# Two of 36 modulation panels moved from the first stage to the routing stage of a two-block transformer kernel

## The reference, cut to what matters

```python
mod  = silu(c) @ w_ada + b_ada                  # block 1: 6 vectors of 1024 (shift, scale, gate, twice)
x   += gate1 * mixer(modulate(x, ...)) @ w_out  # attention heads and delta-rule heads side by side
h    = modulate(x, norm2_w, shift2, scale2)
l    = h @ w_router + b_router                  # 32 experts, the best 4 of each token, softmax weights
x   += gate2 * sum_over_chosen(weight * expert(h))      # expert: 1024 -> 2 x 1024 -> swiglu -> 1024
# block 2, two layers, each:
mod   = silu(c_2)  @ ada_w_2[i] + ada_b_2[i]    # 6 vectors of 1024, for the tokens
mod_c = silu(c_ctx) @ ada_w_2[i] + ada_b_2[i]   # the same weights, for the context rows
# then a mixer (retention; neighbourhood attention) and an MLP of 4096
```

## Time and profile before

| what | value |
| --- | --- |
| median of 3 runs | 2687.79 us (2685.8 to 2687.81) |
| the profiled execution | 2683.9 us |
| its span, first to last instruction | 2682.1 us |
| PE busy / PEld busy | 2512.1 us (94%) / 1846.0 us (69%) |
| DVE / ACT / POOL busy | 1308.6 us (49%) / 500.5 us (19%) / 25.7 us (1%) |
| bytes moved by DMA | 661.33 MB, mean 247 GB/s |
| mean granted TensorE clock | 0.975 |

### The profile page before, as it was taken

The page is one execution under the profiler, slowest core; times in us unless marked ns, Lnnn a source line. Parts: engine busy times, 40 slices in busy tenths (PEclk is TensorE's granted clock), DMA queues, the critical chain, the costliest instruction groups (busy, mean ns, idle before and its releaser), DMA issues.

```text
span 2682.1 us, 44817 instructions
## 1 busy us (share of the span) xinstructions
PE 2512.1 (94%) x18374; PEld 1846.0 (69%) x18374; DVE 1308.6 (49%) x2733; ACT 500.5 (19%) x684; POOL 25.7 (1%) x46
## 2 busy tenths in 40 slices
PE   6997989999999999999989999998999998997998
PEld 5886755655555555555567777776888887775897
DVE  2445543333333333333364535447655456776876
ACT  1111110000000000000022222232222213332442
POOL 0000000000000000000000000000000000000000
PEclk8998989999999999999989999998999999998999
DMA  8789779999999999999942122121322322322652
GB/s 341 293 310 348 299 300 420 422 422 422 422 422 422 422 422 422 422 422 422 421 185 90 63 79 79 63 94 63 111 94 94 98 89 81 119 93 87 220 188 78
DMA packets 94078, 661.33 MB, mean 247 GB/s; under 512 B 10513, under 2 KB 11169, under 8 KB 15985
## 3 DMA queue, kind: packets, MB, share of 16 engines
q1 hardware_dynamic: 89360, 642.10, 60.6%
q0 software_dynamic: 4608, 17.66, 2.0%
HBM read 658.66 MB, written 1.05 MB: 246 GB/s over the span
## 4 chain that ended last, share of the span: by engine, by line
PE 76%; DMA 11%; DVE 8%; issue 2%; SPq 2%; ACT 1%; DVEq 0%; ACTq 0%
PE bank L185 19%; PE bank L1809 9%; DMA diag_gtmp<-in_panels_e 9%; PE bank L1790 9%; PE bank L1677 6%; PE bank L1729 3%; PE bank L1663 3%; PE bank L1272 3%; PE bank L1129 2%; PE bank L1569 2%; DMA ring<-in_units_a 2%; PE bank L1550 2%; SPq L664 2%; PE bank L1708 2%; PE bank L1886 1%
## 5 line engine op out<-in xcount | busy, mean ns | idle before, releaser
L185 PE MATMUL bank<-ring,scratch 128*64 128x256 f32 x2176 | 249.8, 382 | 0.0
L185 PEld LDWEIGHTS bank<-ring,scratch 128*64 128x64 f32 x2176 | 150.2, 137 | 94.9 <-issue 26.2
L927 ACT ACTIVATE scratch<-scratch 128x256 f32<-128x256 f32 x68 | 28.3, 416 | 807.5 <-DVE scratch L2570 807.5
L2574 DVE TENSOR_SCALAR scratch<-bank 128x256 f32<-128x256 f32 x68 | 28.9, 425 | 225.3 <-PE bank L185 225.3
L2931 DVE TENSOR_TENSOR w_lo<-ring,w_hi 128x2048 fp32r<-128x2048 f32 x46 | 105.4, 2291 | 67.5 <-ACT w_hi L1019 67.3
L2570 DVE TENSOR_SCALAR scratch<-bank 128x256 f32<-128x256 f32 x68 | 28.9, 425 | 204.3 <-PE bank L185 204.3
L1790 PE MATMUL bank<-hT_hi,w_hi 128*128 128x512 f32 (+1 forms) x352 | 126.1, 358 | 0.8 <-ACT mtmp L1030 0.8
L185 PE MATMUL bank<-hT,scratch 128*64 128x256 f32 x1088 | 125.5, 381 | 0.0
L1809 PE MATMUL bank<-w_hi,hid_hi 128*128 128x512 f32 x320 | 124.6, 390 | 0.5 <-DVE hid_lo L2939 0.5
L1790 PE MATMUL bank<-hT_hi,w_lo 128*128 128x512 f32 (+1 forms) x352 | 125.1, 355 | 0.0
L1790 PE MATMUL bank<-hT_lo,w_hi 128*128 128x512 f32 (+1 forms) x352 | 125.1, 355 | 0.0
(11 more groups left out here) (544 smaller groups left out, 5147.1 us busy)
## 6 DMA issues: line engine op xcount, KB each, us to landing
ring<-in_panels_e SPq DMA_DIRECT2D x136, 1024.0 KB, 25.6
ring<-in_units_a SPq DMA_DIRECT2D x88, 1024.0 KB, 7.2
hid<-in_panels_e SPq DMA_DIRECT2D x68, 1024.0 KB, 25.3
hT<-in_panels_e SPq DMA_DIRECT2D x68, 1024.0 KB, 25.5
ring<-in_panels_m SPq DMA_DIRECT2D x64, 1024.0 KB, 5.2
yacc<-in_panels_e SPq DMA_DIRECT2D x34, 1024.0 KB, 25.5
diag_gtmp<-in_panels_e SPq DMA_DIRECT2D x34, 1024.0 KB, 26.2
rows<-in_panels_e SPq DMA_DIRECT2D x34, 1024.0 KB, 26.1
```

The source lines that it names most:

```text
L185: m = self.pe.matmul(b[s * rows:(s + 1) * rows, 0:cols], lhs(k), v[:, s * cols:(s + 1) * cols], start=(first and k == 0), stop=(k == KT - 1))
```

## The change

Panels 34 and 35 leave the first stage. All other panels there are taken two places earlier: panel 24 stands where 26 stood, 25 behind level 0, and so on. The two units of each late panel are put behind the units of the output product. The late products are made in the routing: 34 behind the logits, 35 behind the sums over `sel`; their turns come behind the turns of the gathered rows. On DVE, both copies into `arow` stand behind the weights of experts 0 and 1, and both additions to `modcol` behind the scaled rows. SP issues the four late units between expert panels 0, 2 and 4, and the expert panels in the order 0, 2, 4, 5, 1, 3, since slots 1 and 3 are the ring that the late units lie in. Before the output biases PE waits for banks 6 and 7.

```diff
+LATE = 2
@@ first_units
-    add_ada(ADA - 20)
-    return r + [("out", c, h, UNIT) for h in range(2) for c in range(2)]
+    add_ada(ADA - 20 - LATE)
+    r.extend([("out", c, h, UNIT) for h in range(2) for c in range(2)])
+    add_ada(LATE)
+    return r
@@ sync
-            for n, (_, _, _, words) in enumerate(order):
+            late = len(order) - 2 * LATE
+            for n, (_, _, _, words) in enumerate(order[:late]):
...
-            for used, value in ((b2_go, 1), (unit_used, len(order) - 2), (tiles_free, 1), (unit_used, len(order)),
-                                (rows_ready, XT), (tiles_free, 2)):
+
+            def first_panel(used, value, n):
                 sp.wait_ge(used, value)
-                panel(pe_[loads.n], loads, start=True)
+                for h in range(2):
+                    half_panel(pe_[n], n, h)
+                loads.n += 1
+
+            first_panel(b2_go, 1, 0)
+            for n in range(late, late + 2):
+                first_unit(n, UNIT)
+            first_panel(tiles_free, 1, 2)
+            for n in range(late + 2, late + 4):
+                first_unit(n, UNIT)
+            first_panel(rows_ready, XT, 4)
+            first_panel(tiles_free, 2, 5)
+            first_panel(unit_used, late + 2, 1)
+            first_panel(unit_used, late + 4, 3)
@@ tensor
-                if not more:
-                    ada_beside(24)
                 if i:
                     att_turn()
+            AD.read()
+            ada_turn(23, AD)
+            att_values(DN_HEADS - 1)
             ada_product()
-            AD.read()
-            ada_turn(24)
-            att_values(DN_HEADS - 1)
-            ada_before(26)
...
-                ada_before(27 + l)
+                ada_before(25 + l)
...
-            ada_before(34)
+            ada_before(32)
...
-            ada_before(35)
+            ada_before(33)
...
-            ada_turn(ADA - 1)
+            ada_turn(ADA - LATE - 1)
@@ tensor, routing
             S.close(pe.matmul(b[:, EXPERTS:2 * EXPERTS], logit_part[:, 1, :], stack[:, :], start=True, stop=True))
+            ada_product(AD)
             from_dve.get()
...
             S.close(pe.matmul(b[:, 2 * EXPERTS:3 * EXPERTS], ones[:, :], sel[:, 1, :], start=False, stop=True))
+            ada_product(AD)
             G.read()
...
                         pe.wait_ge(b2_in, 16)
+                        AD.read()
                         output_biases(0)
...
             S.read()
+            for j in range(ADA - LATE, ADA):
+                AD.read(1)
+                ada_turn(j, AD)
             fillers = (EG, ES, EA, EM)
@@ vector (the same renumbering, and)
             places((0, 1))
             weights((0, 1))
+            for j in range(ADA - LATE, ADA):
+                ada_product(j, AD)
             turned_gates()
             gathered(0)
             gathered(1)
+            for j in range(ADA - LATE, ADA):
+                ada_turn(j, AD)
             list_started()
```

More of the change, by code:

```diff
@@ L654, in _, with panel @@
         def _(sp):
-            def panel(src, panels, start=False):
+            def panel(src, panels):
                 for h, used in enumerate((E["half0"], E["done"])):
-                    if not start:
-                        sp.wait_ge(used, panels.at(1 - len(wide)))
+                    sp.wait_ge(used, panels.at(1 - len(wide)))
                     half_panel(src, panels.n % len(wide), h)
@@ L2385, in _ @@
                 level_part(p, 0).then_inc(level_ready[p], 1)
-            ada_product(25)
-            ada_turn(24)
+            ada_turn(23, AD)
             att_values(DN_HEADS - 1)
-            ada_before(26)
+            ada_product(24)
             A.settle()
@@ L2404, in _ @@
                     .then_inc(level_ready[p], 1)
-            ada_before(27)
+            ada_before(25)
             for l in range(1, LEVELS):
```

## The result

| | before | after |
| --- | --- | --- |
| median of 3 runs | 2687.79 us (2685.8 to 2687.81) | 2666.2 us (2663.91 to 2668.76) |
| profiled execution, its span | 2683.9, 2682.1 us | 2666.2, 2664.4 us |
| PE / DVE / ACT busy | 2512.1 / 1308.6 / 500.5 us | 2503.6 / 1308.2 / 500.3 us |
| mean granted clock | 0.975 | 0.979 |

The ratio of the runs is 0.9922, 95% interval 0.99 to 0.9945. Forecast was 2672.3 us in a range from 2667.5; measured is 2666.2, so the time lies 1.3 us outside the range on the fast side, and the gain is 21.6 us by the medians and 17.7 by the two profiled executions, for 15.5 forecast.

What follows compares the result with a forecast made beforehand. The experts' fixed DMA stream sets the end, so time won ahead of its issue at 364.24 us is won whole. 13.8 + 2.0 = 15.8, taken as 15.5; 2687.8 - 15.5 = 2672.3 us, range 2667.5 to 2679.5.

Steps and rivals of the forecast that it cites:

- the bound: Experts: streamed at a flat 422 GB/s, 984 us for 198 panels, so their end is the issue at 364.24 plus a constant.
- part 1: First stage without two panels: level 1's second half starts at 236.2 against 250.0, gain 13.8 us, bounds 12.1 to 14.4.
- The reading beside it: First stage near 222 us: panels take 2 us each at full clock and need 5 us of transfer each.
- Rival (a): First stage: only PE's work on two panels is saved, 4.4 us, giving 2683.4 us; chance 0.05.
- Rival (b): Ahead of the experts: the bytes bind, the load stream keeps its length, nothing changes, 2687.8 us; chance 0.04.
- part 2: Routing: the late panels delay little and raise PE's clock by about 350 us; net 2.0 us gained, bounds 1.3 lost to 3.6 gained.
- part 3: SP's queue and the ring: expert panels 1 and 3, issued later, still land in time under idle DMA; cost nothing.
- rival (c): Start of the experts: panels 1 and 3 come late, the kernel is slower, 2695 us at 40 us from issue; chance 0.04.
- the number and the range: Whole kernel: 2672.3 us from a 15.5 us gain on the median, range 2667.5 to 2679.5 us.

Runs made afterwards that it cites:

- e4: The kernel before with two blocks of 32 matmuls on constants (fillers) added in the routing; 2682.23 us against 2682.98, ratio 0.9997.
- e6: The kernel before with all matmuls, but the four units of panels 24 and 25 loaded as 32 KB instead of 1 MB; 2681.48 us, ratio 0.9987.
- e5: The kernel before with all loads, but 8 matmuls for 32 in panels 24 and 26; 2682.89 us against 2685.49, ratio 0.9988.
- e1: The changed kernel measured once more, nothing altered, beside the kernel before; 2668.86 us against 2682.98, ratio 0.9944.
- e12: The changed kernel measured a third time, nothing altered, in a later set on another chip; 2669.04 us against 2683.02, ratio 0.9949.
- e3: The changed kernel with panels 34 and 35 and their loads left out and 32 matmuls on constants in each of their routing places; 2667.42 us, ratio 0.994.
- e2: The changed kernel with panels 34 and 35 left out, with their loads, products, copies and turns, both routing places empty; 2671.47 us, ratio 0.996.
- e11: The changed kernel plus 32 matmuls on constants while ACT writes the first row features and 28 ahead of the first expert; 2664.3 us, ratio 0.994.

## Why the prediction was right and wrong

**Right: the bound.** The experts' stream is a constant. The table's column has 998.6 to 1001.5 us, and the issue of the second round's first half panel carries all that is won ahead of it. That step counted 984 us of transfer and the landing.

**Right: part 1 in size.** Forecast 13.8 us. By the two first profiles the logits came 12.9 us earlier. Part of the missing 0.9 us may be an earlier clock step: in the profile after, panel 21 took 2.70 us at 212, and PE waited 1.04 for panel 23's second unit. Two traces of the first stage of before (before and e4) have their logits at 345.2 in the mean, and the three of the changed kernel at 331.2: 14.0. Panel 25's second unit came at 235.4 for the 234.05 forecast, and full clock held, as taken.

**Right, and shown in part: why it is 13.8.** The sum walked through PE's instructions with the units' landing times held, and that was sound: up to there both kernels ask for the same units. The reading beside it, that panels need 5 us of transfer each, fits the kernel before, where the DMA share is 0.99 and 1.01 from 215 to 235 us and the 12.38 us of the earlier trace rows are the flight of one unit among four. It is not the whole: e6 took 4 MB away and won 3 us, because a unit is asked for only when its slot is free. Rival (a), only PE's work, fell with e5: its work was worth nothing at that place. Rival (b), the bytes, fell with the result, which moved no byte out: 15.5 us gained for none. The Trainium skill, "Perfetto Trace Analysis", Identifying the Most-Contended Engine, by which that rival's time would have come, does not hold over a whole span here. The Trainium skill, "Perfetto Trace Analysis", Optimization Strategy, speaks of kernels with several regimes, in which the most-contended engine changes; the trace before is of that kind: up to 350 us PE is busy for 303 us and the DMA moves 320 GB/s, in the experts the DMA share is 1.01 at 422 GB/s, and what was won lies ahead of the experts.

**Right: part 2, with its spread.** Forecast 2.0 us, bounds -1.3 to 3.6. The first profile showed 4.7, outside; the mean over six traces without and five with fillers is 2.7, inside. I had taken the clock to rise near 350 and the first expert to run at half: that is e1 and e12. The first profile after had full clock in both, the case I had set as an upper bound, with 1 us on top because panel 34 met the rising clock in its middle. That the mean lies so near the forecast is luck in part: the kernel before with the same fillers, e4, gained 1.1 us by the trace and 0.8 by the medians. The traces agree in direction with the Trainium skill, "TensorE: Matmul & The Clock Gate", Part 1, by which activity releases the half rate: e3 reached full clock in the routing and e2 did not before 347. That fillers pay for themselves is shown for e3 against e2 (4.0 us) and not for e4 against before (0.8 us, within the noise).

**Right: part 3.** Expert panels 1 and 3 were not late; PE came to `ring` at 350.66 without a wait, and rival (c) did not occur. e3, without the late loads, is no faster than the changed kernel by its trace, and 1.4 us by the medians, less than either scatters.

**Wrong: the number and the range.** The step that failed is this: "The median of the runs lies 3.9 above that execution, so 2687.8 - 15.5 = 2672.3 us", with "2 us for the spread of the runs". I took the distance between a profiled execution and a median of three as a property of the kernel and carried it over, and took the spread of those three as the spread of executions. In the result that distance is nothing: the changed kernel's profiled execution is itself the median, 2666.2. In 58 runs of the kernel before it is 0.2 (2684.1 for 2683.9), and their standard deviation is 3.1 us with a range of 14. The miss of 6.1 us is these 3.9, and 2.2 by which the two profiled executions differ more than the forecast's 15.5. Those 17.7 are, rounded, 12.9 up to the logits, 4.7 in the routing and 1.1 in the experts, less 0.9 in block 2, which had the same work; the routing's 4.7 for 2.0 is the term that was off in that trace, and 17.8 us of routing instead of 15.8 in e1 and e12 make it 2.6. From the profiled execution alone, 2683.9 - 15.5 = 2668.4, the forecast would have been within 0.3 us of the 2668.6 of all runs. That is luck in part: an execution lies anywhere in that spread, and e1's profiled one is 2.8 us above the median of its six.

Why the first three runs of the kernel before were slow stays open. Only 5 of the 58 later runs lie above 2687.7, and a median of three drawn from them reaches 2687.79 about once in a hundred draws (an estimate), so chance alone is not a good reading. Sets do differ: the kernel before had medians of 2682.98 and 2685.49 us in two sets on one chip and 2683.02 on the other.

## What to carry to other kernels

Where an engine waits at a ring of buffers, ask when a slot comes free as well as how many bytes are on the way, and how many users stand close behind each other: in e6 the wait went from two panels to the next one when their bytes were taken out, and in the changed kernel it nearly went when other work stood between the panels. Work that has to be done somewhere belongs where the engine idles in a chain that another engine sets. A sum of changes against one profiled execution should stay with that execution, and its range needs the spread of executions, which three runs don't show.

## What was not expected of the hardware

- The time of a kernel with PE busy for 94% of its span varies by 0.5% from execution to execution with the same instructions: 2677.3 to 2691.4 us, both ends among the twenty runs of one set on one chip. Where the traces of the changed kernel part in the routing, 15.8 us once and 17.8 twice, it is at steps of the granted clock, in a chain with gaps of 1 to 3 us on PE.
- Matmuls that compute nothing can be worth time: e3 is 4.0 us under e2. With the routing's two gaps filled, by panels or by fillers, the second round's first issue came 2.7 us sooner behind the logits in the mean than with the gaps open (five traces against six), though each filler stands ahead of the chain's next step. In the kernel before they gained 0.8 us, which is within the noise.
- Filling one gap moves the half-rate stretch. In e11 the rows and panel 34 ran at full clock, and panel 35, behind a new wait of 2 us, took 3.39 us for 1.95.
- The flight of a load depends on what else is on the way. In the kernel before one unit of 1 MB took 12.38 us with the DMA engines busy throughout, for a median of 7.2 us over all such units.
